# Two-block transformer on one core: the last four token tiles' norms split between GpSimd and VectorE, the last tile worked by halves of its columns

## The reference, cut to what matters

```python
def rms_norm_2(x, g):
    xf = x.astype(jnp.float32)
    y = xf * lax.rsqrt(jnp.mean(xf * xf, axis=-1, keepdims=True) + EPS)
    return y.astype(x.dtype) * g
...
    x = x + hierarchical_moe(rms_norm_2(x, g_moe[l]), ...)   # each token: two experts, weighted
    return rms_norm_2(x, g_final)
```

## Time and profile before

| what | value |
|---|---|
| median of 3 runs | 2259.02 us (2257.34 to 2260.10) |
| profiled execution, its own time | 2258.34 us |
| its span from first to last instruction | 2256.5 us |
| PE busy | 2217.3 us (98%) |
| DVE busy | 1311.1 us (58%) |
| ACT busy | 1107.7 us (49%) |
| POOL busy | 55.9 us (2%) |

### The profile page before, as it was taken

The page is one execution under the profiler, slowest core; times in us unless marked ns, Lnnn a source line. Parts: engine busy times, 40 slices in busy tenths (PEclk is TensorE's granted clock), DMA queues, the critical chain, the costliest instruction groups (busy, mean ns, idle before and its releaser), DMA issues.

```text
span 2256.5 us, 30145 instructions
## 1 busy us (share of the span) xinstructions
PE 2217.3 (98%) x11051; PEld 1815.6 (80%) x11051; DVE 1311.1 (58%) x1927; ACT 1107.7 (49%) x1645; POOL 55.9 (2%) x70
## 2 busy tenths in 40 slices
PE   9999999999999999999999999999999889999998
PEld 7887888888888876788888888868888778888886
DVE  4567653333374346653333376743455589999898
ACT  3435363433432238362433435364335468888886
POOL 1000000000000000000000000000000010000001
PEclk9999999999999999999999999999999989999999
DMA  6220242323323220242332332302313199999997
GB/s 198 85 79 25 85 131 94 102 93 97 99 73 105 85 84 1 94 131 94 102 94 94 102 112 89 94 29 89 98 66 112 61 351 411 412 412 412 411 412 269
DMA packets 128856, 337.64 MB, mean 150 GB/s; under 512 B 10496, under 2 KB 11680, under 8 KB 128752
## 3 DMA queue, kind: packets, MB, share of 16 engines
q1 hardware_dynamic: 117744, 296.85, 37.0%
q0 software_dynamic: 7840, 27.59, 3.7%
q10 hardware_dynamic: 3168, 11.77, 1.3%
HBM read 320.96 MB, written 15.20 MB: 149 GB/s over the span
## 4 chain that ended last, share of the span: by engine, by line
PE 91%; DVE 6%; ACT 1%; DMA 1%; issue 1%; SPq 0%; DVEq 0%; ACTq 0%; POOLq 0%
PE bank L2405 43%; PE bank L2408 19%; PE bank L2855 11%; PE bank L2897 6%; PE bank L2479 2%; PE bank L2488 2%; PE bank L2572 2%; PE bank L2429 1%; PE bank L2520 1%; DVE w_l L1403 1%; PE bank L2835 1%; DMA spare<-in_w_gate_dram 0%; PE bank L2842 0%; PE bank L2467 0%; DVE stat L1435 0%
## 5 line engine op out<-in xcount | busy, mean ns | idle before, releaser
L1403 DVE TENSOR_TENSOR w_l<-w_raw,w_h 128x1024 fp32r<-128x1024 f32 x370 | 447.4, 1222 | 542.9 <-ACT w_h L846 539.6
L846 ACT CAST w_h<-w_raw 128x1024 fp32r<-128x1024 f32 x370 | 385.8, 1051 | 723.5 <-PE bank L2405 513.9
L2405 PE MATMUL bank<-w_h,xt_h 128*128 128x512 f32 (+1 forms) x960 | 376.0, 392 | 3.2 <-DVE w_l L1403 2.6
L2405 PE MATMUL bank<-w_h,xt_l 128*128 128x512 f32 (+1 forms) x960 | 370.8, 386 | 0.0
L2405 PE MATMUL bank<-w_l,xt_h 128*128 128x512 f32 (+1 forms) x960 | 370.5, 386 | 0.0
L2405 PE MATMUL bank<-w_h,ht_h 128*128 128x512 f32 x624 | 243.9, 391 | 0.7 <-DVE w_l L1403 0.7
L1403 DVE TENSOR_TENSOR w_l<-spare,w_h 128x1024 fp32r<-128x1024 f32 x184 | 220.5, 1220 | 40.3 <-ACT w_h L846 39.8
L2405 PE MATMUL bank<-w_h,ht_l 128*128 128x512 f32 x624 | 242.9, 389 | 0.0
L2405 PE MATMUL bank<-w_l,ht_h 128*128 128x512 f32 x624 | 242.8, 389 | 0.0
L2408 PE MATMUL bank<-xt_h,w_h 128*128 128x512 f32 x608 | 236.6, 389 | 1.1 <-DVE xt_l L1470 1.1
L2408 PE MATMUL bank<-xt_l,w_h 128*128 128x512 f32 x608 | 236.5, 389 | 0.0
(11 more groups left out here) (386 smaller groups left out, 2933.2 us busy)
## 6 DMA issues: line engine op xcount, KB each, us to landing
w_raw<-in_ffn_w_dram SPq DMA_DIRECT2D x128, 512.0 KB, 3.8
spare<-in_w_down_dram SPq DMA_DIRECT2D x92, 512.0 KB, 12.9
spare<-in_w_gate_dram SPq DMA_DIRECT2D x88, 512.0 KB, 12.3
w_raw<-in_w_up_dram SPq DMA_DIRECT2D x88, 512.0 KB, 12.8
w_raw<-in_w_in_dram SPq DMA_DIRECT2D x30, 512.0 KB, 3.8
w_raw<-in_ev_w_in_dram SPq DMA_DIRECT2D x28, 512.0 KB, 3.7
w_raw<-in_od_w_in_dram SPq DMA_DIRECT2D x24, 512.0 KB, 3.8
slot_y_dram<-slot_out ACTq DMA_DIRECT2D x21, 512.0 KB, 6.7
```

Of the source, the lines that this page charges most:

```text
L846: nc.scalar.copy(w_h[:, n % SLOTS, :], raw_of(n)).then_inc(sem("w_hi"), 1)
L1403: V.tensor_tensor(w_l[:, s_, :], raw_of(n), w_h[:, s_, :].bitcast(F32), ALU.subtract)\
L2405: mm = T.matmul(bank[set0 + m][:, 0:g.width], a[:, c, toks_of(m)], b[:, kk, :], start=first, stop=last)
```

## The change

Four things are changed, all in the end.

1. The norms of tiles 0 and 1 move from DVE to POOL, and go to `back[:, i, 0, :]` instead of X: a product of the tile with the gain as soon as `final_x` is there, then a product with the reciprocal of the root. DVE keeps the reciprocals (`inverse_root`) and signals them by `final_rs`.
2. In DVE's order the `gathered(3)` step moves ahead of `picked_up(2)`, into the place of the norm of tile 0.
3. For tile 3, PE signals each bank of 512 columns by itself, DVE adds them by halves (`picked_up_by_halves`), and the norm of tile 3 is two instructions of 512 columns. ACT waits for both halves.
4. SP stores tiles 0 and 1 from `back`, tile 2 from X as before, and tile 3 as two transfers of 512 columns (256 KB each). The order of the queue stays: tile 0, 1, 2, 3.

```diff
             out_v = out[0].rearrange("(t p) d -> t p d", p=P)
-            for i in range(NT):
-                sp.wait_ge(sem("src_ready"), src.start["final"] + i + 1)
-                sp.dma_start(out_v[i], X[:, i, :]).then_inc(sem("stored"), 16)
-            sp.wait_ge(sem("stored"), 16 * NT)
+            for i in range(2):
+                sp.wait_ge(sem("first_normed"), 2 * i + 2)
+                sp.dma_start(out_v[i], back[:, i, 0, :]).then_inc(sem("stored"), 16)
+            sp.wait_ge(sem("src_ready"), src.start["final"] + 1)
+            sp.dma_start(out_v[2], X[:, 2, :]).then_inc(sem("stored"), 16)
+            for half in range(2):
+                cols = slice(half * HALF, (half + 1) * HALF)
+                sp.wait_ge(sem("src_ready"), src.start["final"] + 2 + half)
+                sp.dma_start(out_v[NT - 1][:, cols], X[:, NT - 1, cols]).then_inc(sem("stored"), 16)
+            sp.wait_ge(sem("stored"), 16 * (NT + 1))
...
+            for i in range(2):
+                pool.wait_ge(sem("final_x"), i + 1)
+                nc.gpsimd.tensor_tensor(back[:, i, 0, :], X[:, i, :], FINAL_GAIN, ALU.mult)\
+                    .then_inc(sem("first_normed"), 1)
+                pool.wait_ge(sem("first_normed"), 2 * i + 1)
+                pool.wait_ge(sem("final_rs"), i + 1)
+                nc.gpsimd.tensor_scalar(back[:, i, 0, :], back[:, i, 0, :], rs[:, i:i + 1], None, ALU.mult)\
+                    .then_inc(sem("first_normed"), 1)
...
-                act.wait_ge(sem("final_x"), i + 1)
+                act.wait_ge(sem("final_x"), i + 1 + (i == NT - 1))
...
+            def picked_up_by_halves(i):
+                own.wait()
+                for half in range(2):
+                    cols = slice(half * HALF, (half + 1) * HALF)
+                    dve.wait_ge(sem("late_product"), i + 3 + half)
+                    V.tensor_tensor(X[:, i, cols], X[:, i, cols], banks[:, SUM_BANK[i] + half, :], ALU.add)\
+                        .then_inc(sem("final_x"), 1)
+
+            def inverse_root(i):
+                dve.wait_ge(sem("final_root"), i + 1)
+                V.reciprocal(rs[:, i:i + 1], sd[:, i:i + 1]).then_inc(sem("final_rs"), 1)
+
+            def normalised(i, halves=1):
                 dve.wait_ge(sem("final_root"), i + 1)
                 own.do(V.reciprocal(rs[:, i:i + 1], sd[:, i:i + 1]))
-                V.scalar_tensor_tensor(X[:, i, :], X[:, i, :], rs[:, i:i + 1], FINAL_GAIN, ALU.mult, ALU.mult)\
-                    .then_inc(sem("src_ready"), 1)
+                for half in range(halves):
+                    cols = slice(half * D // halves, (half + 1) * D // halves)
+                    V.scalar_tensor_tensor(X[:, i, cols], X[:, i, cols], rs[:, i:i + 1], FINAL_GAIN[:, cols],
+                                           ALU.mult, ALU.mult).then_inc(sem("src_ready"), 1)
...
             picked_up(1)
-            normalised(0)
+            inverse_root(0)
+            gathered(3)
             picked_up(2)
-            gathered(3)
-            picked_up(3)
-            normalised(1)
+            inverse_root(1)
+            picked_up_by_halves(3)
             normalised(2)
-            normalised(NT - 1)
+            normalised(NT - 1, 2)
...
-                mm.then_inc(sem("late_product"), 1)
+                    if half or i == NT - 1:
+                        mm.then_inc(sem("late_product"), 1)
```

More of the change, by code:

```diff
@@ L2328, in picked_up @@
                     .then_inc(sem("final_x"), 1)
-            def normalised(i):
+            def picked_up_by_halves(i):
[9 more added lines that the diff above has]
+            def normalised(i, halves=1):
                 dve.wait_ge(sem("final_root"), i + 1)
                 own.do(V.reciprocal(rs[:, i:i + 1], sd[:, i:i + 1]))
-                V.scalar_tensor_tensor(X[:, i, :], X[:, i, :], rs[:, i:i + 1], FINAL_GAIN, ALU.mult, ALU.mult)\
-                    .then_inc(sem("src_ready"), 1)
+                for half in range(halves):
+                    cols = slice(half * D // halves, (half + 1) * D // halves)
+                    V.scalar_tensor_tensor(X[:, i, cols], X[:, i, cols], rs[:, i:i + 1], FINAL_GAIN[:, cols],
+                                           ALU.mult, ALU.mult).then_inc(sem("src_ready"), 1)
             late_lo()
```

## The result

The changed kernel takes 2265.62 us (median of 6 runs, 2263.80 to 2270.32) against 2259.56 us of the kernel before (6 runs, 2257.34 to 2261.06). The ratio is 1.0031, with a 95% interval of 1.0021 to 1.0041: slower by 0.31%, and the whole interval lies above 0.2%.

The account below looks back on a forecast made before the run. PE fills nearly all; at the end DVE's chain and the last stores' flow tie. 2244.42 + 3 x 3.1 + 0.1 = 2253.8, + 5.83 = 2259.65, 3.15 us later than 2256.5: forecast 2262.0 us, range 2256.2 to 2267.8.

Parts of the forecast that it names:

- What bounds the end: At the end, tile 1's norm on POOL holds the later stores in SP's queue; 5.83 us from it to the end.
- tile 1 normed: End of tile 1's norm, forecast at 2253.8 on POOL; 0.83 + 4.20 + 0.80 us of stores follow.
- The forecast itself: Three POOL products end to end delay tile 1's stores: end 3.15 us later, time 2262.0 us; chance 0.40.
- the full range: Time from rival A's near top, 2267.8 us, down to 2256.2 for quick POOL products; leaves out about 1 in 10.
- rival A: POOL and two-SBUF-tensor DVE instructions block each other, the later waiting for the whole other: middle 2265.7 us; chance 0.36.
- the forecast's own range: Time 2259 us with POOL instructions of 2.3 us each, to 2264 us with 3.8 us each.
- the prediction's own border of 2263.5 us: Time above which the change counts as slower, from measurements telling about 0.2%, 4.5 us; slower was given 0.40.
- the cost given to the sharing of DVE and POOL: The forecast let DVE and POOL run beside each other at no cost: nothing added.
- 3.1 us for each product: In POOL's chain, each product was taken as three passes of a 1.05 us fill, both kinds alike.
- its two sums: rival A's end: 2266.5 with 3.1 us per POOL product, 2261.2 with 2.05 us; times 2268.3 and 2263.0.
- DVE ends 1.7 us earlier: DVE's last half norm of tile 3 was to end at 2251.75 instead of 2253.45.
- The library load is hidden: The load ahead of POOL's first product was taken as hidden under 8 us of cover.

Follow-up runs that it names:

- e4: The changed kernel with POOL's scalar product written with two multiplications instead of one: ratio 1.0010 to the kernel before; first addition to end 19.38 us against 22.76.
- e9: The kernel before with three POOL products of 1024 columns added behind the last norm, DVE idle: first addition to end 26.32 us against 17.20.
- e3: The changed kernel with SP's store of tile 1 moved behind tiles 2 and 3: ratio 1.0024 to the kernel before; first addition to end 22.62 us.

## Why the prediction was right and wrong

- **What bounds the end: right.** POOL's chain to "tile 1 normed", then 5.83 us. Measured 5.69; e4 moved the end one to one with POOL's products. The stores were not the only thing behind them: POOL's drain ended level with the last store.
- **The forecast itself: too early.** It had the end 3.15 us later, the stretch shows 5.56. The measured 2265.62 us lies in the full range (2256.2 to 2267.8), which was made to take in rival A, and above the forecast's own range, which ended at 2264. By the prediction's own border of 2263.5 us the outcome is slower, to which it gave 0.40. The step that failed is the cost given to the sharing of DVE and POOL: nothing. DVE's second gathered addition took 3.26 us instead of 1.28, and the reciprocal of tile 0, at which POOL's chain starts, came 1.96 us late. The other term is POOL's three products: 9.4 us with the handovers, measured 10.03. That they are so near is luck. By e9 their own lengths are 2.86 + 2.34 + 2.86 = 8.06 us, 1.2 us less than 3 x 3.1; waiting for DVE adds 1.70 (0.86 + 0.84), the handovers 0.27. So of the 5.56 us about 3.7 (1.96 + 1.70) came from the sharing, and by this sum (an estimate, from e9's lengths) the change would have lost about 1.9 us without any.
- **3.1 us for each product: wrong one by one, near in the sum.** The product of two tensors is 2.34 us; by the Trainium skill (GPSIMD Engine Reference, 3.1 Elementwise), with its ratio of 1.96, I had estimated 2.4, and the trace agrees (2.34 is 1.92 times DVE's 1.22). The scalar product is 2.86 us alone and 3.72 in place, so it is the dearer of the two, although it reads less. Counting passes over a fill did not see that.
- **Rival A, given 0.36, was right in kind; its size was partly luck.** Its middle was 2265.7 us, measured 2265.6, but its two sums had the end 4.7 and 10.0 us later, middle 7.3, and the stretch shows 5.56, nearer to the lower. Its order of events was half right: POOL's first product (3.33 us) did wait for DVE and then held the next addition. The norm of tile 2 was held back too, by tile 1's gain product, where A had the gain product wait for the norm; POOL's last product then waited for this norm to end at 2255.50, 0.84 us of its 3.70. It is the rule of the Trainium skill (SBUF — State Buffer, Who interferes with whom), and the trace agrees for the product of two tensors (1.98 and 1.86 us lost beside it). For the scalar product with one operation A's "whole of the other" went too far. The first half norm, at 2255.61, took 1.41 us, the second 0.74, so the first lost 0.67 us and went on at 2256.28, while the product beside it ran 1.93 us more, to 2258.21:

```profile
L2365 DVE SCALAR_TENSOR_TENSOR X<-X,stat,cst x3: 739/1414/3143, 2252.4 to 2256.9; 128x512 f32<-128x512 f32 x2, 128x1024 f32<-128x1024 f32 x1
```

- **DVE ends 1.7 us earlier: wrong, and without effect.** It ended 16.55 us after its first addition (2257.69 - 2241.14) against 14.15 before, and the stores of tiles 2 and 3 would have stood behind tile 1 at either.
- **The library load is hidden: right.** POOL's first product starts at 2242.44, 0.08 us after the addition it waits for ended. The load's row (L841, MODIFY_POOL_CONFIG) stands at 2235.2, so the cover was 7.2 us; how much of it the load used, no run shows.
- **The tail of POOL: not seen at all.** It made no difference to the changed kernel, where it ended level with the last store, but it took back what e3 won.

## What to carry to other kernels

An offload to GpSimd had three prices here beside its own length. A VectorE instruction with two SBUF tensors waited for a GpSimd product beside it (0.5 to 2.0 us), and a GpSimd product for such an instruction that had begun (0.8 to 1.1 us). Everything in a queue behind its result waited. And the program ended no earlier than 5.5 to 5.6 us after GpSimd's last computing instruction. Put such work beside VectorE instructions that read PSUM (they kept their 1.22 us), and let the last of it end at least 5.6 us before the end. And where a limit of the same length lies beside the one in the chain (here the flow of the last three stores), count both before splitting work to shorten one.

## What the runs showed of the hardware that was not expected

- GpSimd's closing drain ended 5.3 to 5.4 us after its last instruction, be it a fill of 128x1 (5.42 us from its start), a product of 128x1, or one of 128x1024 (5.37). In the kernel before, whose GpSimd ended with indirect transfers, it ended at 2240.5, 7.1 us after the last of them was issued (2233.33) and far ahead of the end.
- GpSimd's scalar product of 128x1024 float32 takes 2.86 us with one multiplication and 1.12 us with two, the second by 1.0.
- A GpSimd product with one SBUF tensor held VectorE's instructions of two SBUF tensors back by 0.53 to 0.67 us; that with two held two of them back by 1.98 (3.26 - 1.28) and 1.86 us. VectorE went on 0.2 us before the end of a product of two tensors or of one with two multiplications, but 1.93 us before the end of a scalar product with one. VectorE's additions of PSUM and SBUF, 1.22 us, were not touched.
